# Hybrid decoder layer on one core: the order of the exponent, the rotary rounding and the output addition in attention, the PSUM bank of small turned tiles, and one step of the norm beside the output projection

## The reference, cut to what matters

```python
def attend(i):                                   # 128 queries, all 8 heads
    sc = einsum('bqhd,bkhd->bhqk', qn, k_nope) + einsum('bqhr,bkr->bhqk', qr, k_rope)
    sc = where(causal, sc * scale, -inf)
    p = softmax(sc, axis=-1)
    return einsum('bhqk,bkhd->bqhd', p, v)
...
merged = sigmoid(gate_mla) * o_mla + sigmoid(gate_lru) * o_lru
h = h + _rmsnorm(merged @ w_out, mix_post_g)
h = _half_ffn(h, ...)                            # begins with an RMSNorm of h
```

## Time and profile before

| | us |
|---|---|
| runs, median of 3 | 2250.87 |
| the profiled execution | 2256.11 |
| its span | 2254.3 |
| PE busy in it | 2158.2 (96%) |
| DVE busy | 1366.8 (61%) |
| ACT busy | 984.0 (44%) |
| POOL busy | 414.2 (18%) |

### The profile page before, as it was taken

How to read it: one execution, slowest core, us unless ns; L and a number is a source line. 1 busy time by engine, 2 the same in 40 slices (tenths; PEclk the granted TensorE clock), 3 DMA queues, 4 the chain that set the end, 5 groups by cost and what they waited for, 6 DMA issues and landing times.

```text
span 2254.3 us, 25946 instructions
## 1 busy us (share of the span) xinstructions
PE 2158.2 (96%) x9837; PEld 1790.5 (79%) x9837; DVE 1366.8 (61%) x1715; ACT 984.0 (44%) x1563; POOL 414.2 (18%) x448
## 2 busy tenths in 40 slices
PE   5999999999998999999999888999899999999998
PEld 4888788878886888888888677788688888888886
DVE  6568865557585665311212788677766766547666
ACT  6443333334362777411323666535543333334444
POOL 4123320000032122000011445402203321000002
PEclk8999999999999999999999999899899999999999
DMA  3345452253442211222411100255235453216344
GB/s 121 95 168 178 159 168 67 70 196 102 150 159 80 52 47 48 66 79 71 124 46 30 29 10 10 104 200 201 93 106 184 162 195 121 73 58 222 100 136 154
DMA packets 220293, 249.85 MB, mean 111 GB/s; under 512 B 24261, under 2 KB 161546, under 8 KB 220170
## 3 DMA queue, kind: packets, MB, share of 16 engines
q1 hardware_dynamic: 220170, 248.19, 33.7%
HBM read 192.06 MB, written 55.57 MB: 110 GB/s over the span
## 4 chain that ended last, share of the span: by engine, by line
PE 88%; DVE 5%; ACT 3%; POOL 2%; issue 2%; DMA 0%; SPq 0%; POOLq 0%; ACTq 0%; DVEq 0%
PE ps L88 28%; PE ps L89 28%; PE ps L90 28%; PE ps L2344 1%; PE ps L2312 1%; PE ps L380 1%; POOL a_rot L2229 1%; ACT a_probs L2288 1%; DVE a_pt L98 0%; DVE a_s L2278 0%; ACT w_hi L94 0%; DVE a_rot L2211 0%; DVE w_lo L98 0%; DMA entry_x<-in_x_dram 0%; DVE a_rot L2210 0%
## 5 line engine op out<-in xcount | busy, mean ns | idle before, releaser
L98 DVE TENSOR_TENSOR ff_w_lo<-ff_raw,ff_w_hi 128x512 fp32r<-128x512 f32 x264 | 216.2, 823 | 174.9 <-ACT ff_w_hi L94 174.5
L88 PE MATMUL ps<-ff_t,ff_w_hi 128*128 128x512 f32 x704 | 275.3, 391 | 10.9 <-DVE ff_t L98 10.9
L89 PE MATMUL ps<-ff_t,ff_w_hi 128*128 128x512 f32 x704 | 274.8, 390 | 0.0
L90 PE MATMUL ps<-ff_t,ff_w_lo 128*128 128x512 f32 x704 | 274.6, 390 | 0.0
L94 ACT ACTIVATE ff_w_hi<-ff_raw 128x512 fp32r<-128x512 f32 x264 | 164.7, 627 | 176.7 <-PE ps L90 174.0
L88 PE MATMUL ps<-d_b_hi,d_a_hi 128*128 128x512 f32 x608 | 237.4, 391 | 3.7 <-DVE d_a_lo L98 3.7
L89 PE MATMUL ps<-d_b_lo,d_a_hi 128*128 128x512 f32 x608 | 236.6, 389 | 0.0
L90 PE MATMUL ps<-d_b_hi,d_a_lo 128*128 128x512 f32 x608 | 236.6, 389 | 0.0
L98 DVE TENSOR_TENSOR w_lo<-w_raw,w_hi 128x1024 fp32r<-128x1024 f32 (+2 forms) x81 | 90.4, 1119 | 234.4 <-ACT w_hi L94 234.4
L88 PE MATMUL ps<-ff_b,ff_w_hi 128*128 128x512 f32 x528 | 208.8, 395 | 6.0 <-ACT ff_u2x L715 5.0
L90 PE MATMUL ps<-ff_b,ff_w_lo 128*128 128x512 f32 x528 | 207.6, 393 | 0.0
(11 more groups left out here) (303 smaller groups left out, 4322.9 us busy)
## 6 DMA issues: line engine op xcount, KB each, us to landing
ff_raw<-in_ffn_w_gate_dram SPq DMA_DIRECT2D x44, 512.0 KB, 3.9
ff_raw<-in_ffn_w_up_dram SPq DMA_DIRECT2D x44, 512.0 KB, 4.0
d_sums<-in_ffn_w_down_dram SPq DMA_DIRECT2D x44, 512.0 KB, 4.2
sums_scratch<-d_sums SPq DMA_DIRECT2D x88, 256.0 KB, 2.6
w_raw<-in_w_in_dram SPq DMA_DIRECT2D x32, 512.0 KB, 4.0
d_raw<-sums_scratch SPq DMA_DIRECT2D x24, 512.0 KB, 3.2
w_raw<-in_w_out_dram SPq DMA_DIRECT2D x24, 512.0 KB, 4.0
spill_scratch<-ff_st SPq DMA_DIRECT2D x44, 256.0 KB, 2.8
```

The lines of the kernel that those rows point to most:

```text
L88: pe.matmul(out, lh, rh, start=start, stop=False, skip_group_check=go_on)
L89: pe.matmul(out, lh, rl, start=False, stop=False, skip_group_check=go_on)
L90: return pe.matmul(out, ll, rh, start=False, stop=stop, skip_group_check=go_on)
L98: return nc.vector.tensor_tensor(lo, src, as_f32(hi), ALU.subtract)
```

## The change

Four things, all in the order or place of work; no instruction is added or removed.

1. Turned tiles of s = 0 to 3 alternate between bank 4 (s = 0, 2) and bank 5 (s = 1, 3), where before all four went through bank 4. What PE waits for before it turns a tile follows: s = 2 and 3 wait for the tile two before, s = 4 waits for the one two before in bank 4 and for the one before in bank 5.
2. On ACT the exponent stands ahead of the rotary rounding, and ahead of the pair rounding.
3. On DVE the output addition stands behind the maximum and the rest of the turned tile.
4. In `OUT_STEPS`, step 6 of the last of the three tiles beside group 2 moves from k = 4 to k = 5.

```diff
+    @staticmethod
+    def turn_bank(n, b):
+
+        s = n % HEAD_TILES
+        return 4 + s % 2 if s < 4 else 4 + b
+
+    def bank_before(self, n, b):
+
+        s = n % HEAD_TILES
+        if s in (0, 1):
+            return self.piece(n - 1 - s, s) if n > s else None
+        if s in (2, 3):
+            return self.piece(n - 2, 0)
+        if s == 4:
+            return self.piece(n - 2 + b, 0)
+        return self.piece(n - 1, b)
...
         for b in self.pieces(n):
-            if b == 0 and n > 0:
-                pe.wait_ge(self.S["pt_split"], self.piece(n - 1, 0) + 1)
-            if b == 1 and n >= HEAD_TILES or b == 1 and s > 4:
-                pe.wait_ge(self.S["pt_split"], self.piece(n - 1 if s > 4 else n - 5, 1) + 1)
+            before = self.bank_before(n, b)
+            if before is not None:
+                pe.wait_ge(self.S["pt_split"], before + 1)
...
         if n >= 2:
             self.turned_hi(act, n - 2)
+        if n < HEADS * HEAD_TILES:
+            self.exponent(act, n)
+            if n > 0 and self.beside(n - 1):
+                self.rope_act(act, self.beside(n - 1))
         if s == 3 and h > 0 and h % 2 == 0:
             self.pair_hi(act, h // 2 - 1, slice(0, SEQ), 2 * h)
...
-            if n > 0 and self.beside(n - 1):
-                self.rope_act(act, self.beside(n - 1))
-            self.exponent(act, n)
-            if self.beside(n):
-                self.unit_act(act, self.beside(n))
+        if n < HEADS * HEAD_TILES and self.beside(n):
+            self.unit_act(act, self.beside(n))
...
     def dve_step(self, dve, n):
         h, s = n // HEAD_TILES, n % HEAD_TILES
+        if n < HEADS * HEAD_TILES:
+            self.maximum(dve, n)
+        if n >= 2:
+            self.turned_lo(dve, n - 2)
         if s == 7:
             self.add(dve, h, 0)
         if s == 3 and h > 0:
             self.add(dve, h - 1, 1)
-        if n < HEADS * HEAD_TILES:
-            self.maximum(dve, n)
-        if n >= 2:
-            self.turned_lo(dve, n - 2)
...
-             ((0, 0, 0, 0, 1, 2, 2, 3, 3), (0, 0, 1, 1, 2, 3, 3, 4, 4), (0, 0, 1, 1, 2, 4, 4, 5, 5)))
+             ((0, 0, 0, 0, 1, 2, 2, 3, 3), (0, 0, 1, 1, 2, 3, 3, 4, 4), (0, 0, 1, 1, 2, 4, 5, 5, 5)))
```

More of the change, by code:

```diff
@@ L2305, in turn @@
         for b in self.pieces(n):
-            if b == 0 and n > 0:
-                pe.wait_ge(self.S["pt_split"], self.piece(n - 1, 0) + 1)
-            if b == 1 and n >= HEAD_TILES or b == 1 and s > 4:
-                pe.wait_ge(self.S["pt_split"], self.piece(n - 1 if s > 4 else n - 5, 1) + 1)
+            before = self.bank_before(n, b)
+            if before is not None:
+                pe.wait_ge(self.S["pt_split"], before + 1)
             for j in range(4 * b, min(4 * b + 4, s + 1)):
                 at = s - j if b else j
-                last = pe.transpose(c.ps[:, 4 + b, at * P:(at + 1) * P], self.prob(n)[:, j * P:(j + 1) * P], c.ident[:, :])
+                last = pe.transpose(c.ps[:, self.turn_bank(n, b), at * P:(at + 1) * P], self.prob(n)[:, j * P:(j + 1) * P], c.ident[:, :])
             last.then_inc(self.S["t_done"], 1)
@@ L2320, in turned @@
         first = 4 - count if b else 0 if s < 4 else 4
-        return x[:, first:first + count, s % 4, :], self.c.ps[:, 4 + b, 0:count * P].rearrange("p (j q) -> p j q", q=P)
+        return x[:, first:first + count, s % 4, :], self.c.ps[:, self.turn_bank(n, b), 0:count * P].rearrange("p (j q) -> p j q", q=P)
     def turned_hi(self, act, n):
```

## The result

The changed kernel takes 2257.47 us, median of 11 executions (2255.06 to 2259.43), against 2253.23 for the kernel before beside it. The ratio is 1.0017, 95% interval 1.0010 to 1.0025: 3.8 us more, where 2.1 less had been forecast. The time is above the predicted range (to 2257) by half a microsecond. The profiled execution took 2258.64 us with a span of 2256.8, against 2256.11 and 2254.3 before.

What follows compares the result with a forecast made beforehand. TensorE was taken as the bound, busy 96% of the span, so only its idle time or low clock could yield gains. Terms -5.0 + 1.5 + 0.6 - 0.6 - 0.3 + 1.7 = -2.1 us took 2250.87 to 2248.8, range 2241 to 2257.

Steps and rivals of the forecast that it cites:

- projection: End of output projection: TensorE's 3.27 us wait goes whole, plus 1.7 us of low clock behind it; -5.0 us.
- odd heads, three: Heads 1, 3, 5: savings at waits used up by later rotary rounding and addition; +0.5 us each, +1.5 in all.
- even heads, three: Heads 2, 4, 6: wait at s = 2 goes, but late pair rounding delays step 6's scores; +0.2 each, +0.6 us.
- head 0: Scores of step 4: exponent no longer waits behind the rotary rounding; 0.7 us gained, less 0.1 for the addition: -0.6.
- head 7: Last head, which has no units: its small waits partly go; -0.3 us.
- clock: New 2 us stands before step 6's scores in even heads lower TensorE's clock; one head of three, +1.7 us (0 to 5.1).
- The slower one: Rival: new stands in heads 1 to 6 cost 1.7 us of low clock each, 10.2 us; time 2257.3, chance 0.14.
- the waits come through in full: Rival: each attention wait that loses its cause counts fully, 10.6 us; with the projection 2235.3 us, chance 0.14.
- the projection's wait only shrinks: Rival: the wait shrinks or is replaced, so -5.0 becomes about 0; +2.9 us, 2253.8, chance 0.12.

Runs made afterwards that it cites:

- e1: Kernel before with only the changed step numbers of the output projection; 2249.40 us, ratio 0.9982.
- e10: Changed kernel plus products nobody reads, in the waits before the scores of step 6 (heads 2, 4, 6) and at the start of heads 1 to 6; ratio 0.9992.
- e11: Kernel before plus products nobody reads, in the waits at s = 2 (heads 2, 4, 6) and at the start of heads 1 to 6; ratio 0.9994.
- e13 to e15: With fillers: kernel before, exponent first (1.0008); changed kernel, rotary rounding ahead again (0.9980); kernel before, projection, banks, pair rounding behind exponent (1.0017).
- e5: Changed kernel plus eight products nobody reads in the wait before the scores of step 6 in heads 2, 4 and 6; 2254.27 us, ratio 1.0004.
- e3: Kernel before with only the two banks for the small turned tiles; 2251.60 us, ratio 0.9997.
- e9: Changed kernel with the rotary rounding ahead of the exponent again; 2260.82 us, ratio 1.0035.
- best version: Kernel before with the projection's step numbers, two banks and fillers in heads 0 to 7; 2243.99 us, ratio 0.9958.
- e4: Kernel before with only the exponent put ahead of the rotary rounding; 2261.31 us, ratio 1.0039.

## Why the prediction was wrong

The chains over ACT and DVE came nearly as forecast. What failed is the step from the late maximum to TensorE in the even heads; the clock term was too small as well, and head 0's gain did not come.

| term | forecast | measured | from |
|---|---|---|---|
| projection | -5.0 | -5.1 (trace), -4.1 (e1) | traces, e1 |
| odd heads, three | +1.5 | +1.8 | e10 - e11 |
| even heads, three | +0.6 | +3.9 | e10 - e11 |
| head 0 | -0.6 | 0 | e10 - e11 |
| head 7 | -0.3 | -0.7 | e10 - e11 |
| clock | +1.7 | +4.2 | 5.6 - 1.4, fillers in e10 and e11 |
| sum | -2.1 | +4.1 (time: +3.8) | |

The heads' terms are read from one trace of each kernel. The clock term is a difference of four ratios and uncertain by about 3.3 us, from 1 to 7.5. The forecast time was missed by 8.7 us (2257.47 against 2248.8), and 2.4 of these are not the change: three executions gave 2250.87 for the kernel before, eleven beside the changed one gave 2253.23.

- **Even heads, the failed step.** I set the new scores of step 6 (12.49 after the head's start for the maximum, 14.29 for the scores, in the terms of the last table) against where they stood in the earlier trace rows, 13.92, and called it 0.4 late. The maximum did come late as worked out, even 0.4 more (12.87). But 13.92 was no place that the chain set: its row has no wait. At full clock the kernel before has these scores at 13.18, with its maximum at the same 11.4. The prediction's sentence that the slow stretch of head 4 "lies where the DVE chain sets the time, so full speed there wins nothing" was wrong: there TensorE was late by 0.74 us because of its clock. So a comparison point that held a clock loss was taken for structure. 14.64 - 13.18 is 1.46 us where 0.4 was forecast: 0.74 by the comparison point and 0.35 by the chain. I let 0.3 of the 0.4 be taken back by later waits; of the 1.46, 0.1 to 0.2 were, and 1.3 stay in the head.
- **Which edits do it** is shown by e13 to e15: the exponent ahead of the rotary rounding +0.42, the pair rounding behind the exponent together with the late addition +0.85 (the pair rounding alone puts the maximum 1.7 late). The two add up to e10's 1.3. The late addition alone was not run.
- **The clock term.** I took one head of three. The traces have 0.88, 0.94 and 0.88 in all three, each behind its stand of 2.3 us, and head 1 at 0.94 behind the 1.86 us at its start. The measured 4.2 lies inside the bounds that were given (0 to 5.1). The trace before also had clock losses that the change could take away: the prediction read heads 3 and 4 and took the others as their repeats, but head 6 is at 0.87 and 1.15 us longer than head 4, and head 7 is at 0.86 and 3.0 us longer than the changed kernel's. By time, fillers in the 2.3 us stands take 2.9 us off the changed kernel (e5), and those at the head starts the rest of the 5.6.
- **Odd heads** held: +0.41 to +0.73 for a forecast +0.5, with the waits of 0.93 us before the scores, 0.48 for POOL and 0.39 before the fifth transpose that use up what was won.
- **Head 0.** Its wait of 1.49 us in the earlier trace rows is gone before the scores of step 4, but one of 0.92 us has come before those of step 5, and the head is as long as before (21.87 us against 21.93).
- **The rivals.** The slower one had the right side and nearly the right time (2257.3), but not the right sum: it put 10.2 us down to clock, where about 4.2 are clock, and structure is 5.0 against my 1.2. That its time came so near is in part luck, since it starts from the 2250.87. That the waits come through in full is excluded by e3, which removes 1.49 and 1.01 us waits and gains nothing. That the projection's wait only shrinks is excluded by e1, whose stretch there is 5.1 us shorter.

The Trainium skill, "Perfetto Trace Analysis", section "Matmul Optimizations", says that the matmul engine scales its power with utilisation, so that matmuls should run back to back. The runs agree, as far as the granted clock tells it, and give it a size here: holding the engine busy in its waits takes 5.6 us off the changed kernel and 12.4 off e9's order; the 1.4 of the kernel before are not clear of the noise.

**Open.** Why e9's order, with stands of 0.41 and 2.28 us in an even head, loses so much more clock than the changed one, with 0.95 and 2.28, is not settled; the single traces show where the clock was low, not why there.

## What to carry to other kernels

Before a position in a trace is used as the point from which a change is counted, ask whether the clock was low just ahead of it: a place that the clock set is not a place that the chain set, and it hides a delay of the same size. Removing a wait in a closed loop over several engines may only move it (e3), and longer or fewer waits can cost by the clock behind them as much as by themselves. Where TensorE must stand, work that nobody reads, placed in the wait and shorter than it, told structure from clock here, and may stay in the kernel: with it the best version is 9.5 us under the kernel before, some 4 of them from the projection.

## What was not expected of the hardware

- More work, put into TensorE's waits, made the kernel faster: by 4.3, 5.6, 7.0 and 12.4 us in four versions, and by 1.4, which is inside the noise, in a fifth. Head 0, at 0.76 to 0.84 in every trace without fillers of its own, went to 1.00 and 1.8 us shorter.
- The length of a wait alone does not tell what the clock does behind it. In the changed kernel a wait of 1.86 us has eight transposes behind it at 1.83 us in head 1, while at 1360.00, behind 1.87 us, they take 1.06:

```profile
1276.78 1.83 PE L2328 MATMUL ps<-ident,a_probs 128*128 128x128 f32 x8 [1.86 <-DVE a_pt L98]
```

- One profiled execution can mislead by more than the effect. e4's took 2254.47 us, the shortest of its twelve (median 2261.31), and e3's shows attention 5 us shorter than the kernel before's (198.1 against 203.1) where the times differ by nothing. The mean granted clock of each execution stands beside its time: 0.986 in both of these, against a mean of 0.983 over e4's executions.
